# GpSimd takes the rotation's products and the scaling of exponentials in a two-layer decoder step

## The reference

```python
def rope_partial(x, pos, rot_dim):
    ...
    out = jnp.concatenate([x1 * cos - x2 * sin, x1 * sin + x2 * cos, rest], axis=-1)

def dsa_attend(q, qi, wi, qpos, kidx, gather_kv, topk):
    ...
    dots = jnp.einsum('bthd,bsd->bths', qi, kidx) * (IDX_DIM ** -0.5)
    score = jnp.einsum('bth,bths->bts', wi, jax.nn.relu(dots))
    admissible = jnp.arange(n_keys)[None, None, :] <= qpos[None, :, None]
    top_val, sel = lax.top_k(jnp.where(admissible, score, -jnp.inf), topk)
    ...
    p = jax.nn.softmax(logits, axis=-1)
    out = jnp.einsum('btkgs,btskd->btkgd', p, v_sel)
```

## Time and profile before

| what | value |
| --- | --- |
| median of 3 runs | 856.08 us (854.96 to 859.27) |
| the profiled execution | 855.14 us, its span 853.6 us |
| granted clock of TensorE, mean | 0.979 |
| TensorE busy | 804.7 us, 94% |
| VectorE, ACT, GpSimd busy | 240.2, 118.4, 137.4 us |
| moved | 227 MB, mean 266 GB/s |

### The profile page before, as it was taken

One profiled execution on the slowest core, in us unless ns is written; L12 is line 12 of the kernel. 1 busy time (PEld: TensorE's weight loads), 2 busy tenths in 40 slices (PEclk: granted clock), 3 DMA queues, 4 the chain that ended last, 5 costly groups with the idle time before them and its releaser, 6 DMA issues.

```text
span 853.6 us, 13331 instructions
## 1 busy us (share of the span) xinstructions
PE 804.7 (94%) x5633; PEld 533.2 (62%) x5633; DVE 240.2 (28%) x692; ACT 118.4 (14%) x302; POOL 137.4 (16%) x229
## 2 busy tenths in 40 slices
PE   7999999999999999999967869999998999999995
PEld 5888878888888888877655446853443343343432
DVE  0173215000000000074665761264222021021025
ACT  0020113000000001131202543131000010000010
POOL 3400584424000000011100301004111001010120
PEclk9999999999999999999988969999999999999998
DMA  9899998899540049999223732949999999999971
GB/s 273 279 390 379 326 271 280 301 312 313 179 136 1 0 136 350 219 230 188 94 104 111 273 139 107 411 173 355 374 410 390 411 394 410 396 390 411 397 275 51
DMA packets 112426, 227.00 MB, mean 266 GB/s; under 512 B 25074, under 2 KB 64298, under 8 KB 109172
## 3 DMA queue, kind: packets, MB, share of 16 engines
q1 hardware_dynamic: 96580, 177.13, 58.9%
q0 software_dynamic: 12048, 42.47, 14.5%
q10 hardware_dynamic: 3744, 6.62, 2.1%
HBM read 203.03 MB, written 23.17 MB: 265 GB/s over the span
## 4 chain that ended last, share of the span: by engine, by line
PE 77%; SPq 9%; DMA 6%; DVE 5%; issue 1%; ACT 1%; DVEq 0%; ACTq 0%
PE ps L696 47%; PE ps L1185 9%; SPq L355 9%; PE ps L747 3%; PE ps L1213 3%; DMA scr<-moe_w 2%; DMA slot<-moe_w 2%; PE ps L1252 2%; PE ps L1122 1%; PE ps L999 1%; PE ps L1058 1%; DMA slot<-w_in_even 1%; DVE slot L1833 1%; PE ps L875 1%; PE ps L1013 1%
## 5 line engine op out<-in xcount | busy, mean ns | idle before, releaser
L696 PE MATMUL ps<-rw,slot 128*128 128x264 f32 x640 | 142.6, 385 | 0.0
L696 PEld LDWEIGHTS ps<-rw,slot 128*128 128x128 f32 x640 | 120.8, 189 | 21.6
L696 PE MATMUL ps<-xw,slot 128*128 128x264 f32 x512 | 127.8, 406 | 6.1 <-DMA slot<-w_in_even 6.1
L1185 PE MATMUL ps<-slot,hT 128*32 128x512 f32 x1104 | 121.5, 592 | 4.7 <-DMA slot<-moe_w 4.5
L696 PEld LDWEIGHTS ps<-xw,slot 128*128 128x128 f32 x512 | 99.5, 198 | 27.3 <-DMA slot<-w_in_even 8.7
L1185 PEld LDWEIGHTS ps<-slot,hT 128*32 128x32 f32 x1104 | 36.4, 110 | 85.0 <-issue 77.2
L696 PE MATMUL ps<-hT,slot 128*128 128x264 f32 x352 | 79.4, 387 | 0.0
L696 PEld LDWEIGHTS ps<-hT,slot 128*128 128x128 f32 x352 | 66.6, 190 | 12.5 <-DVE xw L1584 1.3
L1213 PE MATMUL ps<-slot,hT 128*32 128x256 f32 x1216 | 68.3, 380 | 0.2 <-DMA slot<-moe_w 0.2
L696 PE MATMUL ps<-yT,slot 128*128 128x264 f32 x256 | 59.5, 388 | 0.0
L1213 PEld LDWEIGHTS ps<-slot,hT 128*32 128x32 f32 x1216 | 38.2, 110 | 26.1 <-issue 1.0
(11 more groups left out here) (438 smaller groups left out, 800.7 us busy)
## 6 DMA issues: line engine op xcount, KB each, us to landing
slot<-moe_w SPq DMA_DIRECT2D x50, 1024.0 KB, 19.5
slot<-moe_w SPq DMA_DIRECT2D x16, 2048.0 KB, 22.5
slot<-ffn_w SPq DMA_DIRECT2D x22, 1024.0 KB, 13.6
scr<-moe_w SPq DMA_DIRECT2D x14, 1024.0 KB, 20.1
slot<-ffn_w SPq DMA_DIRECT2D x8, 1408.0 KB, 7.1
slot<-w_in_even SPq DMA_DIRECT2D x4, 2048.0 KB, 16.0
r_rows<-silu ACTq DMA_DIRECT2D x1, 6144.0 KB, 31.4
slot<-k_pages SPq DMA_DIRECT2D x6, 1024.0 KB, 6.5
```

The lines of the kernel that those rows point to most:

```text
L696: mm = pe.matmul(out, lhs(k), rhs(k), start=(k == 0), stop=(k == n - 1))
L1185: mm = pe.matmul(ps[t][32 * j:32 * j + 32, :].rearrange("p (w n) -> p w n", w=2), xgT[:, cap * k + 32 * t:cap * k + 32 * t + 32], moe_slab ...
```

## The change

Four things change.

1. GpSimd makes both products, x cos and x sin. TensorE turns the second one, and VectorE only adds. (R only moves and negates channels whose sines are equal.)
2. GpSimd scales the exponentials by the reciprocals of their sums, before TensorE transposes them. The four spreading products a step and VectorE's multiply go. GpSimd also copies the sample queries (four small copies), and issues one gather of V behind each of the first eight scalings.
3. The digits of the search are spread: one column sum in or behind each query projection group, instead of two in each of the last three. The first digit starts one group earlier, and three digits lie in the head loop's start instead of two. Selection rounds of the prompt move back.
4. VectorE masks a step's logits first and takes the step before's reciprocals behind that, half by half; the tie steps move one step back. ACT loads the Exp table ahead of its waits.

```diff
@@ rotation, GpSimd @@
-                pool.tensor_tensor((mean, rstd)[q % 2][:], hT[:, n, :], rope[:, 0, :], ALU.mult).then_inc(cosd, 1)
+                pool.tensor_tensor((mean, rstd)[q % 2][:], hT[:, n, :], rope[:, 0, :], ALU.mult)
+                pool.tensor_tensor(silu[:, q % 2, :], hT[:, n, :], rope[:, 1, :], ALU.mult).then_inc(cosd, 1)
@@ GpSimd behind the rotation @@
-            for par in range(2):
-                pool.wait_ge(k_mm, 4 * par + 4)
-                for b in range(par, TS, 2):
-                    gather_v(b)
+            def scale_probs(u, half):
+                t = u // 4
+                L = P * (t + 1)
+                col = 32 + 4 * (u % 4) + half
+                row_ = S[u % 2][:, half, :, 0:L]
+                pool.wait_ge(rs_done, 2 * u + half + 1)
+                pool.tensor_tensor(row_, row_, stat[:, col:col + 3:2].unsqueeze(2).to_broadcast([P, 2, L]),
+                                   ALU.mult).then_inc(scaled_done, 1)
+
+            pool.wait_ge(roped, len(ROPED))
...
+                    ins = pool.tensor_copy(qw[rows, j, :, at], q[rows])
+            ins.then_inc(qw_done, 1)
+            pool.wait_ge(qw_done, 1)
+            for u in range(8):
+                for half in range(2):
+                    scale_probs(u, half)
+                    if u < 4:
+                        b = 4 * (u % 2) + 2 * half + u // 2
+                        pool.wait_ge(k_mm, 4 * (u // 2) + 4)
+                        gather_v(b)
@@ TensorE, rotate @@
-                if q < 4:
-                    pe.wait_ge(biased, q + 1)
-                else:
-                    pe.wait_ge(group_free, G_OIN + g + 1)
+                pe.wait_ge(cosd, q + 1)
...
-                pe.matmul(ps[4][:, 0:T], rot, hT[:, n, :], start=True, stop=True).then_inc(rot_done, 1)
+                pe.matmul(ps[4][:, 0:T], rot, silu[:, q % 2, :], start=True, stop=True).then_inc(rot_done, 1)
@@ TensorE, query projections @@
-                oin(wq[i // 4], i % 4, mid=(lambda: tally(2 * i - 10)) if i > 4 else None)
+                oin(wq[i // 4], i % 4, mid=(lambda: tally(i - 4)) if i > 5 else None, at=(6, 4)[i % 2])
+                if i in (4, 5):
+                    tally(i - 4)
...
-                if i in (5, 6):
-                    tally(2 * i - 9)
...
+            tally(4)
             rotate(QQ + 7, 17)
@@ TensorE, probs_t and values @@
-                pe.wait_ge(exp_done, v + 1)
+                pe.wait_ge(scaled_done, v + 1)
...
-                pe.wait_ge(rs_done, u + 1)
-                for c in range(2):
-                    for half in range(2):
-                        col = 32 + 4 * (u % 4) + 2 * c + half
-                        mm = pe.matmul(ps[7][64 * half:64 * half + 64, 256 + P * c:256 + P * c + P],
-                                       stat[:, col:col + 1].to_broadcast([P, 64]), ident, start=True, stop=True)
@@ TensorE, ahead of and in the head loop @@
+            k_logits(0, 0)
             tally(5)
-            k_logits(0, 0)
-            tally(6)
             k_logits(0, 1)
-            tally(7)
...
                 if u == 0:
+                    tally(6)
                     k_logits(1, 1)
+                    tally(7)
@@ ACT @@
+            act.activation(gate[:, 3, :], eps[:, 0:1].to_broadcast([P, 3]), ACT.Exp)
             act.wait_ge(even_stored, 16 * 3)
@@ VectorE, turn @@
-                link(V.tensor_tensor(var[:], ps[4][:, 0:T], rope[:, 1, :], ALU.mult))
-                dve.wait_ge(cosd, q + 1)
-                V.tensor_tensor(hT[:, n, :], (mean, rstd)[q % 2][:], var[:], ALU.add).then_inc(roped, 1)
+                V.tensor_tensor(hT[:, n, :], ps[4][:, 0:T], (mean, rstd)[q % 2][:], ALU.add).then_inc(roped, 1)
@@ VectorE, query projections @@
-                if 5 <= i < 8:
-                    refine(2 * i - 10)
-                    radix(2 * i - 9)
+                if 4 <= i < 8:
+                    refine(i - 4)
+                    radix(i - 3)
+                if 4 <= i < 6:
+                    select(1, (range(3, 5), range(5, 8))[i - 4])
@@ VectorE, shares @@
-                dve.wait_ge(exp_done, 2 * u + 2)
-                col = 4 * (u % 4)
-                V.reciprocal(stat[:, 32 + col:36 + col], stat[:, 16 + col:20 + col]).then_inc(rs_done, 1)
+                for half in range(2):
+                    dve.wait_ge(exp_done, 2 * u + half + 1)
+                    col = 4 * (u % 4) + half
+                    V.reciprocal(stat[:, 32 + col:35 + col:2], stat[:, 16 + col:19 + col:2]).then_inc(rs_done, 1)
@@ VectorE, head loop @@
             for u in range(8):
-                shares(u)
-                if u:
-                    heads(u - 1)
                 if u < 6:
                     masked_logits(u + 2)
+                if u < 7:
+                    shares(u + 1)
                 if u == 0:
+                    refine(6)
+                    radix(7)
+                    refine(7)
+                if u == 1:
                     link(V.tensor_scalar(eqk, X, kth, 0.0, ALU.is_equal, ALU.add, accum_out=sst[:, 4:5]))
...
```

More of the change, by code:

```diff
@@ L610, in _ @@
                 cosine(q, q + 3)
-            for par in range(2):
-                pool.wait_ge(k_mm, 4 * par + 4)
-                for b in range(par, TS, 2):
-                    gather_v(b)
+            def scale_probs(u, half):
[7 more added lines that the diff above has]
+            pool.wait_ge(roped, len(ROPED))
+            for j in range(2):
+                q = hT[:, QQ + 4 * j:QQ + 4 * j + 4, TP:T].rearrange("p x b -> p b x")
+                for half in range(2):
+                    at = slice(16 + 8 * j + 4 * half, 20 + 8 * j + 4 * half)
+                    rows = slice(64 * half, 64 * half + 64)
+                    ins = pool.tensor_copy(qw[rows, j, :, at], q[rows])
[8 more added lines that the diff above has]
+                        gather_v(b)
             pool.wait_ge(so_done, 1)
@@ L687, in bank, with group @@
                 return ps[(done.phase + done.k) % NB]
-            def group(lhs, rhs, n, m=P, ready=None, mid=None):
+            def group(lhs, rhs, n, m=P, ready=None, mid=None, at=4):
                 out = bank()[0:m, 0:T]
                 for k in range(n):
-                    if mid and k == n // 2:
+                    if mid and k == at:
                         mid()
@@ L1964, in _ @@
             ins.then_inc(so_done, 1)
-            heads(7)
             def part(c):
```

53 lines of the change are left out of this document (17 added, 36 removed).

## The result

The changed kernel takes 860.82 us, the median of 20 runs (858.16 to 863.78); the kernel before, beside it, 855.73 (853.46 to 859.27). The ratio is 1.0057, 95% interval 1.0044 to 1.0069: slower by some 5 us, where 850.5 was forecast and 844 to 860 was the range. The profiled execution took 861.09 us (span 859.5, granted clock 0.971 over the span).

The account below looks back on a forecast made before the run. It took TensorE, busy 94% of the span, as the bound, with gaps in the odd layer's projection and attention. Terms +1.9 -11.8 -0.4 +13.5 -5.4 -0.5 +0.5 = -2.2, with 2.4 more -4.6: 850.5 us, range 844 to 860.

Parts of the forecast that it names:

- The first turn's 1.9 us: At the first rotation, TensorE would wait for GpSimd's second product: a cost of 1.9 us.
- Pair 4: Head loop, first to second transposes of the fifth two-heads-per-half group: 5.7 us against 11.1, a gain of 5.4.
- a ring of transposes, masks, reciprocals and scalings: Head loop, pair 0's second transposes to pair 4's first: each waits for GpSimd's scaling; 12.95 us before, loss 13.5.
- The gain of the projections: Query projections up to the first logits: spread column sums cut waits from 12.8 to 5.2 us, a gain of 11.8.
- The first logits to pair 0: From the first logits to pair 0's second transposes: 11.4 us against 11.8, a gain of 0.4.
- the 3.3 us for the clock: Head loop, pairs 0 to 3: transposes and logits at the lower clock while TensorE idles half the time, adding 3.3 us.
- the stretch to the output projection: From pair 4's second transposes to the output projection: 25.9 us before, 1.5 added for a slow start, gain 0.5.
- I took off 2.4 us: Whole sum: the layout applied to the old program ended 1.3 us late; assumed over-counting lowered the forecast by 2.4.
- the 0.5 us for the tie steps: VectorE's sums that overlap GpSimd cost 0.58 us instead of 0.43, so 0.5 us was added.
- the stage: Odd layer's projection and attention, through the output projection, the only part expected to change: 4.6 us shorter.
- A: GpSimd's scaling in the head loop costs 2.5 times the assumed price, 1.8 and 3.6 us: 863 us, chance 0.12.
- B: Lower clock holds from the last projections to the sample values: 7.5 us more, 858 us, chance 0.25.

Follow-up runs that it names:

- ties_wait: Changed kernel in which VectorE waits for the next pair's second scaling before the tie steps that read two on-chip tensors, after pairs 2 and 3; 861.97 us.
- logits_early: Changed kernel with the logits of pair u+2 moved on TensorE from behind pair u's second transposes to ahead of its first ones; 851.64 us.
- shares_first: Changed kernel with the reciprocals of pair u+1 put ahead of the masked logits of pair u+2 on VectorE; 850.60 us.
- dve_scale: Changed kernel with the scaling of the exponentials on VectorE, directly behind each reciprocal, instead of on GpSimd; 860.30 us.

## Why the prediction was wrong

**Right.** The first turn's 1.9 us (1.89). Pair 4: 5.59 us where 5.7 was forecast. That the loop would lose through a ring of transposes, masks, reciprocals and scalings, and that waits for GpSimd would show it, though pair 1 has none and the others are up to 5.65 us, not 1 to 3. The gain of the projections: -8.8, in place of -9.9 with the first turn's cost. The first logits to pair 0 gained 2.5 where I had 0.4, an error of 2.1 us the other way.

**The step that failed** is the sum of the ring: "transposes 0.36, first half of the next logits 0.33 (0.54 wide, half of 1.14)", and the scalings at 0.72 and 1.44. No half of the logits was done at half time: the masks began at 482.62, after all 2.08 us, which was the wide piece at the lower clock. 0.54 stood for 2.2 in pairs 2 and 3. From 2 to 3 I had 6.5 us and it was 10.11, of which 2.3 were the held scaling and the rest these logits and the clock; from 3 to the first of 4 it was 7.83 against 5.4. With the 3.3 us for the clock the loss was to be 13.5, it was 17.2. If those 3.3 us are taken as doubled transposes and logits (an estimate), two terms made the 3.7: the logits took 2.2 us in place of 1.08, twice, which is 2.2 more; and from the first scaling of pair 3 to its second transposes it was 4.41 us where 2.68 stood (two scalings and a gather), and the first wide scaling took some 2.0 in place of 1.44, together 2.3 more. The other pieces gave 0.8 back. So the held scaling weighs as much as the logits. In ties_wait the 2.3 us of the scaling held in pair 3 are gone, but the tie steps take as much more at pair 4. The steps 0 to 1 and 1 to 2 (6.76 and 5.45 us against 6.0 and 5.3), with narrow logits at the full clock, were nearly right.

**The same step behind pair 4.** I let two rings be covered by what follows and put -0.5 for the stretch to the output projection; it was +2.15. logits_early points to the same piece: with the logits out of the ring this stretch is 22.03 us (forecast 25.4). But it falls by 6.0 us, more than the 2.65 that my forecast missed, and its granted clock is 1.00 there from 505 to 520 us against 0.73, so logits and clock aren't told apart. That its pair 0 to 4 is 26.50 (forecast 26.5) and its time 851.64 (forecast 850.5) is in part luck: it has no logits in the ring at all, and it keeps the scaling of 2.59 us that the forecast lacked.

**A term without a row behind it.** I took off 2.4 us because my layout of the program before ended late, half of it by extrapolation. No such over-count shows: apart from the first logits to pair 0 and the 0.5 us for the tie steps, of which nothing shows, every term erred to the short side or was right. Together: the stage was to be 4.6 us shorter and was 2.5 longer. Of these 7.1 us, 3.7 are the ring, 2.65 the stretch behind pair 4, 2.4 this term and 1.1 the projections, less 2.1 and 0.5. The other 3.2 of the 10.3 us between forecast and median lie outside the stage or in the drift between executions.

**The rivals.** A (the scaling costs 2.5 times as much) was wrong in the operation's own price and right, by the interfaces that it named, where VectorE was in the way. A scaling took 0.61 to 0.64 us (256 elements) and 1.04 (512), less than the 0.72 and 1.44 that I took. Beside the scan it took 2.59, beside the compare and the sum two took 4.06:
```profile
495.51 1.27 DVE L1938 SCALAR_TENSOR_TENSOR slot<-slot,sst 128x1032 f32<-128x1032 f32 x1
495.61 4.06 POOL L618 TENSOR_TENSOR scr<-scr,fin 128x512 f32<-128x512 f32 x2 [4.64 <-DVE fin L1908]
496.82 1.95 DVE L1940 TENSOR_TENSOR cache<-cache,slot 128x1032 f32<-128x1032 f32 x1
```
In shares_first, where none is held, the narrow ones take 622 ns on the mean and the wide ones 1042. My argument against A, that the 15 products all took 0.74 to 0.76, missed who is held: those that lay beside a sum of two tensors on VectorE had started first. The kernel before already had a sum on VectorE that started 0.14 us behind a product on GpSimd (381.13) and took 0.89 us in place of 0.43:
```profile
381.27 0.89 DVE L1773 TENSOR_TENSOR hT<-mean,var 128x264 f32<-128x264 f32 x1 [0.28 <-POOL mean L580]
```
B (the lower clock through the loop, 858) was nearest in size, and the clock of 0.61 to 0.73 from 475 to 520 us is in its sense, though from 465 to 475 us it was 1.00. But B named TensorE's pieces in general and not the logits between the transposes and the masks, and it held that the wait's length comes from the clock; two calls in another order take 9 us from pairs 0 to 4 at a clock that is still low.

What is left open: how much of the 5.1 us between the medians is the stage's 2.5, what the low clock costs by itself, above all behind pair 4, and whether the masks could have been split to start on one half of the logits, which wasn't tried.

## What to carry to other kernels

When an operation is put between producer and consumer, follow the order of the queue in front of it before its price: here the reciprocal stood behind the next pair's masks, these behind the next logits, these behind the last transposes, and so two pairs of look-ahead became none; the first fix is to let the hand-over pass what it doesn't need. When a ring is laid out from rows, take every piece as a whole at the clock that the ring itself will leave, and ask of a "half" whether a consumer was ever seen to start on it. And a saving on an engine that only looks busy (15 products of 0.43 us on VectorE) is worth its place on the path, which here showed as nothing (846.40 us with 14 of them moved, 846.75 with none).

## What the runs showed of the hardware

VectorE and GpSimd hold each other up in some pairs of operations. Beside the scan (two tensors from on-chip memory, 2.29 us) a scaling of 0.61 took 2.59; beside the compare and the sum, two of 1.04 took 4.06, and the sum itself took 1.95 in place of 1.22. In the kernel before it was VectorE that came second and was held (0.89 us in place of 0.43, at 381.27). Beside VectorE's counting step, which reads one tensor (477.27 to 478.54), a scaling took 0.61, and in shares_first a wide one that began 0.10 us behind a mask (489.23 to 489.90), which reads one operand from the matmul's banks, took its 1.04. The Trainium skill bears on this (GPSIMD Engine Reference, section 1. Specifications): the interfaces are shared with VectorE, and contention is with its 2-port modes or with two SBUF inputs. The trace agrees, and shows that beside the scan the scaling waited for nearly the whole of the other's operation: 2.59 is 0.61 and most of the 2.29.

GpSimd's scaling, whose second operand is repeated along the row, took less per element than its product of two full tensors: 0.61 us for 256 and 1.04 for 512 elements against 0.74 for 264. On VectorE the same scaling takes 0.42 and 0.69 (dve_scale).
